# Attention in pairs: both heads of a chunk on the same queries, four score banks, longer lags, no constant gate product

## The reference, cut to what matters

```python
def mem_attend(q, k, v):
    s = jnp.einsum('blhd,bmhd->bhlm', q, k).astype(jnp.float32) * MEM_SCALE
    p = jax.nn.softmax(s, axis=-1).astype(v.dtype)
    return jnp.einsum('bhlm,bmhd->blhd', p, v)

# fox, for one block of 128 queries
s = jnp.einsum('bqhd,bkhd->bhqk', qb, k).astype(jnp.float32) * FOX_SCALE
s = s + jnp.swapaxes(fqb, 1, 2)[..., None] - Fk_t      # F[query] - F[key]
s = jnp.where(kpos[None, :] <= qpos[:, None], s, -jnp.inf)
p = jax.nn.softmax(s, axis=-1).astype(v.dtype)
return jnp.einsum('bhqk,bkhd->bqhd', p, v)
```

## Time and profile before

| | |
|---|---|
| median of 3 runs | 1389.19 us (1388.21 to 1390.13) |
| span of the profiled execution | 1383.9 us, 24787 instructions |
| the same execution's own time beside its span | not recorded; the runs' median is 5.3 us above the span |
| mem attention of layer 0 | from 115.1 us, first output projection matmul at 141.9 |
| mem attention of layer 1 | from 783.2 us |
| fox attention | first scores at 807.6, first output projection matmul at 896.0 |
| mean granted TensorE clock | 0.995 |

### The profile page before, as it was taken

How to read it: one execution, slowest core, us unless ns; L and a number is a source line. 1 busy time by engine, 2 the same in 40 slices (tenths; PEclk the granted TensorE clock), 3 DMA queues, 4 the chain that set the end, 5 groups by cost and what they waited for, 6 DMA issues and landing times. The chain is left out here.

```text
span 1383.9 us, 24787 instructions
## 1 busy us (share of the span) xinstructions
PE 1354.2 (98%) x9956; PEld 1294.2 (94%) x9956; DVE 601.8 (43%) x1087; ACT 495.3 (36%) x869; POOL 37.2 (3%) x60
## 2 busy tenths in 40 slices
PE   6999999999999999999999899999999999999997
PEld 6997999999999999999999766699999999999997
DVE  4756444434444433335644454454444434432221
ACT  6556342222222222225743554434222222221221
POOL 1000000000000000011001100000000000000000
PEclk9999999999999999999999999999999999999999
DMA  6332222322223122243343300022232222223231
GB/s 213 98 103 94 59 80 77 90 77 80 87 76 87 54 84 84 83 135 100 120 108 98 108 1 1 1 77 77 77 91 76 84 83 76 83 61 93 92 101 35
DMA packets 202182, 114.31 MB, mean 83 GB/s; under 512 B 5291, under 2 KB 198475, under 8 KB 202120
## 3 DMA queue, kind: packets, MB, share of 16 engines
q1 hardware_dynamic: 198088, 101.24, 25.0%
q0 software_dynamic: 3840, 12.15, 2.4%
q10 hardware_dynamic: 192, 0.06, 0.0%
HBM read 106.54 MB, written 6.90 MB: 82 GB/s over the span
## 5 line engine op out<-in xcount | busy, mean ns | idle before, releaser
L1060 DVE TENSOR_TENSOR WL<-RAW,WH 128x1024 fp32r<-128x1024 f32 (+3 forms) x209 | 233.8, 1118 | 620.8 <-ACT WH L821 620.7
L821 ACT ACTIVATE WH<-RAW 128x1024 fp32r<-128x1024 f32 (+3 forms) x209 | 203.7, 975 | 518.8 <-PE ACCP L1248 518.7
L1248 PE MATMUL ACCP<-XH,WH 128*128 128x288 f32 x1664 | 360.9, 299 | 5.3 <-DVE XL L1064 5.2
L1248 PE MATMUL ACCP<-XH,WL 128*128 128x288 f32 x1664 | 357.6, 297 | 0.0
L1248 PE MATMUL ACCP<-XL,WH 128*128 128x288 f32 x1664 | 357.2, 297 | 0.0
L1248 PEld LDWEIGHTS ACCP<-XH,WH 128*128 128x128 f32 x1664 | 270.0, 190 | 7.5 <-DVE WL L1060 3.8
L1248 PEld LDWEIGHTS ACCP<-XH,WL 128*128 128x128 f32 x1664 | 269.1, 189 | 0.0
L1248 PEld LDWEIGHTS ACCP<-XL,WH 128*128 128x128 f32 x1664 | 269.1, 189 | 0.0
L1248 PE MATMUL ACCP<-HH,WH 128*128 128x288 f32 (+1 forms) x1104 | 238.2, 298 | 0.0
L1248 PE MATMUL ACCP<-HH,WL 128*128 128x288 f32 (+1 forms) x1104 | 236.6, 296 | 0.0
L1248 PE MATMUL ACCP<-HL,WH 128*128 128x288 f32 (+1 forms) x1104 | 236.5, 296 | 0.0
(11 more groups left out here) (220 smaller groups left out, 1068.2 us busy)
## 6 DMA issues: line engine op xcount, KB each, us to landing
RAW<-in_w_gu SPq DMA_DIRECT2D x88, 512.0 KB, 3.7
RAW<-in_w_down SPq DMA_DIRECT2D x32, 384.0 KB, 3.4
RAW<-in_w_down SPq DMA_DIRECT2D x32, 320.0 KB, 3.1
RAW<-in_w_in SPq DMA_DIRECT2D x16, 512.0 KB, 4.0
RAW<-in_w_mem_kv SPq DMA_DIRECT2D x16, 512.0 KB, 3.9
RAW<-in_w_out SPq DMA_DIRECT2D x16, 512.0 KB, 4.1
RAW<-in_w_kv SPq DMA_DIRECT2D x8, 512.0 KB, 3.6
XR<-in_x_prompt SPq DMA_DIRECT2D x4, 512.0 KB, 6.1
```

The costliest lines, as they stand in the source:

```text
L821: a.activation(WH[:, q % SPLIT_SLOTS, 0:nk, 0:ncol], RAW[:, q % RAW_SLOTS, 0:nk, 0:ncol], ACT.Copy).then_inc(hi_ready, 1)
L1060: v.tensor_tensor(WL[:, q % SPLIT_SLOTS, 0:nk, 0:ncol], RAW[:, q % RAW_SLOTS, 0:nk, 0:ncol], WH[:, q % SPLIT_SLOTS, 0:nk, 0:ncol], ALU.sub ...
L1248: ins_ = t.matmul(ACCP[0:ncol, g % 2, b, 0:c1_ - c0_], w[:, q, k, 0:ncol], m[:, k0 + k, c0_:c1_], start=first and k == 0 and n == 0, stop= ...
```

## The change

Units go in pairs. For fox a pair is the two heads of a chunk on the same query block; for mem two neighbouring query blocks of one head; the sample's units come first, heads in twos, into one bank for all chunks. In a round of the list PE issues the scores of both units of pair n, then the transposes of pair n-2, then the values of pair n-3. In fox the two heads alternate: in scores one product each, in values one product each per block of keys. The matmuls that add F[query] (L1388) are left out.

Scores now use all four banks of MISC (two pairs), the transposes two banks of ACCP, the values the other two, by turns for each chunk. PR has six buffers, PT four. The reciprocal is one instruction for a pair. HH and HL of the sample are written once for four chunks. On DVE the round is: both maxima, HL of a closed chunk, then the scaling of pair n-1; on ACT: HH of a closed chunk, then exp and PT copy for each unit by turns. The output projection waits once for the last PT copy, and in layer 1 takes its k in the order 4 to 7, 0 to 3 (mem first). STG1 moves to another address.

```diff
+        def chunk(kind, tiles, c, pairs):
+            bank = take("bank")
+            for n, pair in enumerate(pairs):
...
+                twos.append(Step(kind="two", rows=units, first=not twos, last=n == len(pairs) - 1, layer=layer,
+                                 j=bank, c=c, t=tiles, att=kind))
...
+            if kind == "mem":
+                chunk(kind, TT, base_c, [[(h, TT), (h + 1, TT)] for h in heads if h % 2 == 0])
+                for h in heads:
+                    branch_bank[layer, base_c + h] = chunk(kind, 0, base_c + h, [[(h, t), (h, t + 1)] for t in range(0, TT, 2)])
+            else:
+                chunk(kind, TT, base_c, [[(h, TT), (h + 1, TT)] for h in heads if h % 2 == 0])
+                for c in range(len(heads) // 2):
+                    branch_bank[layer, c] = chunk(kind, 0, c, [[(2 * c, t), (2 * c + 1, t)] for t in range(TT)])
...
+        for n in range(len(twos) + 4):
+            new, scaled, turned, valued, closed = (lag(n, by) for by in range(5))
+            if closed and closed.last:
+                add("branch_hi", two=closed)
+            if new:
+                add("scores", two=new, m=before["jobs"], s=before["s"], g=before["g"])
+            if closed and closed.last:
+                add("branch_lo", two=closed)
+            if scaled:
+                add("scale_probs", two=scaled)
+            for e in range(2):
+                if new:
+                    add("exp", r=new.rows[e])
+                if turned:
+                    add("turn_probs", r=turned.rows[e], first=turned.first and e == 0, g=before["g"])
+            if valued:
+                add("values", two=valued, g=before["g"])
...
-        PR = place("PR", [P, 3, 512], F32, a0)
+        PR = place("PR", [P, 6, 512], F32, a0)
...
-        PT = place("PT", [P, 2, 512], F32, b0)
+        PT = place("PT", [P, 4, 512], F32, b0)
...
+        def scores_bank(r):
+            return MISC[0:r.nq, (r.u // 2) % 2, r.u % 2]
+
+        def turned_bank(r, g):
+            return ACCP[:, g % 2, r.u % 2]
+
+        def values_bank(j, layer):
+            return ACCP[:, (attend_g[layer] + 1) % 2, j % 2]
...
+            u, nq = two.rows[0].u, two.rows[0].nq
+            dve.wait_ge(probs_ready, u + 2)
+            v.reciprocal(STAT[0:nq, 2, u % 4:u % 4 + 2], STAT[0:nq, 1, u % 4:u % 4 + 2]).then_inc(recip_ready, 1)
...
-                        for k in range(0, r.nk, P):
-                            n = min(P, r.nk - k)
-                            t.matmul(S[:, k:k + n], FP[:, fq:fq + r.nq], SEL[:, r.h, 0:n], start=False, stop=False)
...
+                    if two.rows[0].u >= 4:
+                        pe.wait_ge(probs_ready, two.rows[0].u - 2)
...
+                                t.matmul(scores_bank(r)[:, k0:k0 + n], q, k_, start=part == 0, stop=False)
+                        for r in two.rows:
+                            S = scores_bank(r)
+                            f0 = 0 if r.t < TT else L
+                            t.matmul(S[:, 0:r.nk], SEL[:, r.h, 0:r.nq], NFP[:, f0:f0 + r.nk], start=False, stop=False)
+                            t.matmul(S[:, r.nk - r.nq:r.nk], IDB[:, 0:r.nq], MASK[:, 0:r.nq], start=False,
+                                     stop=True).then_inc(scores_ready, 1)
...
+                        for k in range(nt):
+                            for r in two.rows:
+                                last = value(r, k, nt)
...
+                        order = [HC, HC + 1, HC + 2, HC + 3, 0, 1, 2, 3] if s.which == "out" and s.layer == 1 else None
+                        if first and s.which == "out":
+                            pe.wait_ge(pt_ready, s.units)
```

More of the change, by code:

```diff
@@ L55, in __init__ @@
                  which=None, nsub=None, final=None, body=None, z=None, rjob=None, j=None, att=None, u=None,
-                 h=None, e=None, per=None, nq=None, nk=None, last=None):
+                 h=None, e=None, per=None, nq=None, nk=None, last=None, two=None, rows=None, units=None):
         self.kind = kind
@@ L97, in __init__ @@
         self.last = last
+        self.two = two
+        self.rows = rows
+        self.units = units
 def encoder_kernel(nc, ins, outs):
@@ L178, in resid @@
     def resid(layer, which, nsub, pbase):
[L180 removed]
+        f = dict(units=count["unit"], layer=layer, which=which, nsub=nsub, p=pbase, g=take("acc", KC), o=count["store"],
                  final=layer == DEPTH - 1 and which == "down", body=4 if nsub == 1 else 2)
@@ L201, in attend @@
     def attend(layer, branches):
[L203 to L232, removed]
+        twos = []
@@ new lines, in chunk @@
+        def chunk(kind, tiles, c, pairs):
+            bank = take("bank")
+            for n, pair in enumerate(pairs):
+                units = []
+                for h, t in pair:
+                    keys = MT_TOK if kind == "mem" else (P * (t + 1) if t < TT else PAST + LS)
+                    per = 1 if kind == "mem" else 2
+                    units.append(Step(kind="unit", att=kind, u=take("unit"), h=h, t=t, c=h // per, e=h % per, per=per,
+                                      nq=P if t < TT else LS, nk=keys, layer=layer, j=bank))
+                twos.append(Step(kind="two", rows=units, first=not twos, last=n == len(pairs) - 1, layer=layer,
+                                 j=bank, c=c, t=tiles, att=kind))
+            return bank
@@ L575, in moving_of @@
                     "m": (MH, ML, ml_ready, MT_TOK)}[kind]
+        def scores_bank(r):
[4 more added lines that the diff above has]
+            return ACCP[:, (attend_g[layer] + 1) % 2, j % 2]
+        attend_g = {s.two.layer: s.g for s in steps if s.kind == "scores"}
         BUF = {"q": ZQ, "fq": FQ, "mk": MKT, "fk": FK}
@@ L1233, in _, with product @@
             t = nc.tensor
-            def product(p, g, nk, ncol, hi, lo, width, k0, first, last, per=0, i=0, ready=None, r=None):
+            def product(p, g, nk, ncol, hi, lo, width, k0, first, last, per=0, i=0, ready=None, r=None, order=None):
                 pe.wait_ge(lo_ready, at(p + 1, per, i))
@@ L1239, in product @@
                 hv = halves(width)
-                for k in range(nk):
-                    if r is not None and k == nk - 2:
+                order = order or range(nk)
+                for at_, k in enumerate(order):
+                    if r is not None and at_ == nk - 2:
                         sum_of_squares(r)
@@ L1418, in _, with value @@
-                    for k, (vk, n) in enumerate(tiles):
-                        last = t.matmul(o, vk, PT[0:n, r.u % 2, k * P:k * P + r.nq], start=k == 0, stop=k == len(tiles) - 1)
-                    last.then_inc(pv_done, 1)
+                            return [(VT[:, k, cols], P) for k in range(r.t + 1)]
+                        return [(CFV[:, k, cols], P) for k in range(PK)] + [(VT[0:LS, TT, cols], LS)]
+                    def value(r, k, n_tiles):
+                        rows = slice(0, P) if r.att == "mem" else slice(r.e * FD, (r.e + 1) * FD)
+                        vk, n = tiles_of(r)[k]
+                        c0_ = r.t * P if r.t < TT else r.c * LS
+                        return t.matmul(values_bank(two.j, two.layer)[rows, c0_:c0_ + r.nq], vk,
+                                        PT[0:n, r.u % 4, k * P:k * P + r.nq], start=k == 0, stop=k == n_tiles - 1)
@@ new lines, in _ @@
+                    nt = len(tiles_of(two.rows[0]))
+                    if two.att == "mem":
+                        for r in two.rows:
+                            for k in range(nt):
+                                last = value(r, k, nt)
+                            last.then_inc(pv_done, 1)
+                    else:
+                        for k in range(nt):
+                            for r in two.rows:
+                                last = value(r, k, nt)
+                                if k == nt - 1:
+                                    last.then_inc(pv_done, 1)
```

166 lines of the change are left out of this document (81 added, 85 removed).

## The result

The change takes the kernel from 1388.95 to 1348.07 us (medians of 4 runs each, 1347.0 to 1348.23 after): a ratio of 0.9709 with a 95% interval of 0.9697 to 0.972.

A forecast was written before the change was run, and what follows sets the result against it. TensorE's own queue was taken as the bound. Terms -6.0 - 9.0 - 9.8 - 5.7 + 0.3 + 2.4 + 1.0 = -26.8 took the span from 1383.9 to 1357.1, median 1362.4 us; 8-in-10 range 1354 to 1373.

The forecast's parts named there:

- What bounds the kernel: TensorE's own queue, busy 98% of a 1383.9 us span, so time can only come out of it.
- Shape changes: Fox on PE: three steps between matmuls of different row or column shape cost 0.20 + 0.10 + 0.15 = 0.45 us a unit.
- wait of PE in memory attention: PE waits there for the scaled probabilities (L656), 0.91 us a head.
- Gate product, -6.0: Fox scores: 104 matmuls of L1388 go, 0.058 us each on PE's path, with no shape change: -6.0 us.
- Units in pairs, -9.0: Fox on PE: shape changes once a pair, 20 rounds instead of 40 at 0.45 us: -9.0, range 7 to 10.
- Four banks and memory attention, -5.7 and +0.3: Memory attention loses 7.3 us of waits, sample pairs add 1.6: -5.7; one more pair in flight at attention's start: +0.3.
- Alternating halves, -9.8: Fox scores and values of two heads overlap on array halves: 1.2 and 1.24 us a chunk, upper bound -9.8.
- DVE's order, +2.4: Fox, round of the 512-key pair: PE waits for the scaling behind reduces and HL, 0.4 to 0.6 a chunk: +2.4.
- The end, +1.0: End of layer 1: the last pair's 512-key chain, 2.6 us, has only some 1.6 us of cover: +1.0.
- Span to median: Median of runs lies 5.3 us above the profiled span, so a span of 1357.1 becomes 1362.4.

The follow-up runs named there:

- The pairs of one head: Changed kernel, but a fox prompt pair is two neighbouring query blocks of one head, values by head: 1364.18 us, ratio 0.9824.
- the values by head: Changed kernel, but fox values take all key blocks of one head, then all of the other: 1352.66 us.
- an order of the blocks that eases both: Changed kernel with each fox chunk's query blocks in the order 1, 3, 2, 0: 1345.94 us, and 1345.34 when run again.
- moving HL alone: Changed kernel with HL of a closed chunk put behind the scaling on DVE instead of ahead of it: 1348.01 us.

## Why the prediction was wrong, step by step

- **What bounds the kernel:** right. Shape changes and the wait of PE in memory attention were read from the timeline, and what the change was to take from both is gone in the size that I read.
- **Gate product, -6.0:** right. 5.7 by the head's period in the kernel before; 5.4 (by the ratios) to 6.3 by putting it back.
- **Units in pairs, -9.0:** right. 0.47 us a round saved instead of 0.45, 9.5 in all.
- **Four banks and memory attention, -5.7 and +0.3:** near. Layer 0 gave 26.7 - 23.6 = 3.1 us. Layer 1 reached its first fox scores after 21.0 us instead of 24.4, and after 19.5 in an execution of the same kernel in which the clock took nothing (last section). Of these 5 us about 2 are no gain, an estimate: with pairs more transposes and values of mem stand behind that mark than before (four and six units instead of two and three, at 0.22 and 0.43 us). That leaves some 3 a layer, 6 in all against 5.4.
- **Alternating halves, -9.8: the step that failed.** I called it an upper bound and it was not one. In scores I let one pass of four overlap, from the order of the queue; it is two of four, as four passes take 1.13 us and two took 1.12. In values I held starts at least 0.076 us apart, from four 64-column passes in one half, and that holds within one half only: sixteen passes of two halves take 1.09 us, the last 0.28, so starts are 0.054 apart on the mean. The pairs of one head measured 4.04 us a chunk for the prompt. The sample adds by its rows about 1.0: four passes 64x64 take the 0.65 us that two took, and eight value passes the 0.45 that four took. Four chunks: 20, in place of 9.8. The difference of 10 is the miss of the span: 37.3 against 26.8. With it the rows close: -5.7 - 9.5 - 20.2 - 6 + 1.5 (clock) + 2.4 + 0.6 (next two steps) = -36.9.
- **DVE's order, +2.4:** right in place and size: transposes wait for the scaling in the round after the 512-key scores, 0.39, 0.66 and 0.66 us, and the same 0.66 is in the 1.41 of the last chunk, 2.4 in all. What stood behind it I had not seen: the PT copy on ACT is late by the same half a microsecond, so that curing the one gives nothing.
- **The end, +1.0:** near in size, wrong in place. I had the 512-key pair wait at the end; its transposes at 855.71 wait for nothing. The wait is a round earlier, for the 384-key pair (854.28), whose scaling stands behind the 512-key maxima and HL while no next scores cover it. Beyond DVE's 0.66 it costs 0.75 us, of which some 0.2 were there before.
- **Span to median:** my sum was made against a span of 1383.9 that lay 5.3 under the median. The changed kernel's four runs lie 1.6 over their spans (1348.23 and 1346.6 for the profiled one). So 3.6 of the 40.9 us are in no row. That the profiled execution of before was one of its quick ones is likely: 25 later runs of that kernel have both numbers on record, and all lie 1.6 to 3.4 over their spans, with times down to 1385.64; its own time was not recorded.
- **Two rules of the Trainium skill:** "TensorEngine Tiling (Array Packing)", Key Properties, says that tiles work in parallel; the rows agree, fully, for float32 in two passes. "TensorE: Matmul & The Clock Gate", Part 3, says that matmuls start and end strictly in order; the starts in the values by head do not agree (8 passes in 0.66 us), and the measurement decides. I had worked out my sum by that order without naming it as a rule to be doubted, and so gave "more than my bound" no rival and no chance of its own, only 3 us at the edge of a range for value starts of 0.053 us, about what was measured; for scores I allowed nothing more.

## What to carry to other kernels

Where two products of 64 rows, or of 64 output partitions, lie on different halves of the array, pair them: for the float32 products here the second is free, and it needs no exact alternation as long as the runs of one half stay within four passes of one shape. Count the changes of shape in a round, not the matmuls: each costs 0.1 to 0.2 us, and doing two units between them halves the bill. And look at who is second in line before moving the one that is late; here DVE and ACT were late together, and an order of the blocks that eases both gave what moving HL alone could not. A bound taken from the queue's order is an assumption, and belongs among the rivals.

## What the runs showed of the hardware that was not expected

- **Matmuls pass one another between halves**, three waiting ones: 8, 12 and 16 value passes by head take 0.66, 1.14 and 1.58 us, where alternating takes 0.66, 0.88 and 1.09. Where a run of another shape stands between, none is passed (1.26 us for a sample pair by head, 0.65 alternating).
- **The clock at the head of layer 1's attention.** In the changed kernel's profiled run the window 779.8 to 783.3 has a granted clock of 0.54, nearly all at the 1.2 GHz level, and the eight sample passes take 3.48 us; in a later profiled run of the same kernel they take 1.94, at 1.00. Before them PE had waited 2.32 us for DVE and 0.84 for a copy on ACT, in both. So some executions pay 1.5 us there and some do not, and a single profile is not good to better than that.
